# A float32 block on one TensorE: in units whose input is already whole, the high-weight products first, the low-weight products behind them

## The reference

```python
u = rmsnorm(x, norm_mix) * (1 + scale1) + shift1
aq, ak, av, bq, bkv, biq, bik, biw, cq, ck, cv, g = split_cols(u @ w_in)
y_a, y_b, y_c = diff_attention(...) @ w_br_a, dsa_attention(...) @ w_br_b, moba_attention(...) @ w_br_c
x = x + gate1 * ((sigmoid(g)-weighted sum of y_a, y_b, y_c) @ w_o)
x = x + gate2 * (square(relu(u2 @ w_ff1)) @ w_ff2)
...                                     # second block, two layers:
m = even_mixer(h) or odd_mixer(h)       # convolution and scan, or gated linear attention
h = layer_norm(ALPHA * h + m)
h = layer_norm(ALPHA * h + memory_cross_attention(h, mem, w_q, w_k, w_v, w_o))
h = layer_norm(ALPHA * h + square(relu(h @ w1)) @ w2)
```

## Time and profile before

| | |
|---|---|
| median of 3 runs | 2654.69 us (2653.97 to 2657.85) |
| the profiled execution | 2652.46 us |
| its span, first to last instruction | 2650.7 us |
| mean granted clock of TensorE | 0.992 |
| busy: PE, PEld, DVE, ACT, POOL | 98%, 81%, 56%, 44%, 16% of the span |
| HBM | 94 GB/s over the span |

### The profile page before, as it was taken

One profiled execution on the slowest core, in us unless ns is written; L12 is line 12 of the kernel. 1 busy time (PEld: TensorE's weight loads), 2 busy tenths in 40 slices (PEclk: granted clock), 3 DMA queues, 4 the chain that ended last, 5 costly groups with the idle time before them and its releaser, 6 DMA issues.

```text
span 2650.7 us, 34332 instructions
## 1 busy us (share of the span) xinstructions
PE 2595.9 (98%) x13569; PEld 2147.1 (81%) x13569; DVE 1493.1 (56%) x2875; ACT 1161.1 (44%) x2243; POOL 428.6 (16%) x508
## 2 busy tenths in 40 slices
PE   7999999999999999999999999999999999999998
PEld 5776677798888977887897988889788887888888
DVE  5176877565433389887774743335635744643334
ACT  4356554354232334554654542324533544542324
POOL 0133333100000045553000100000000100100000
PEclk8999999999999999999999999999999999999999
DMA  7342234434433333213421333332320432333331
GB/s 252 110 106 72 64 104 113 119 95 122 124 96 96 89 87 88 64 56 91 133 80 56 88 96 96 96 96 74 88 79 25 131 116 61 90 92 93 94 96 64
DMA packets 468976, 251.35 MB, mean 95 GB/s; under 512 B 15582, under 2 KB 463666, under 8 KB 468815
## 3 DMA queue, kind: packets, MB, share of 16 engines
q1 hardware_dynamic: 466260, 242.56, 32.0%
q0 software_dynamic: 1840, 5.59, 0.7%
q10 hardware_dynamic: 715, 1.01, 0.1%
HBM read 247.00 MB, written 2.13 MB: 94 GB/s over the span
## 4 chain that ended last, share of the span: by engine, by line
PE 86%; DVE 7%; ACT 3%; issue 3%; POOL 1%; DMA 0%; SPq 0%; DVEq 0%; POOLq 0%; ACTq 0%
PE ps L976 20%; PE ps L980 20%; PE ps L978 20%; PE ps L900 3%; PE ps L896 3%; PE ps L898 3%; DVE ps L2595 3%; PE ps L1130 1%; PE ps L914 1%; PE ps L916 1%; PE ps L1472 1%; PE ps L1494 1%; PE ps L927 1%; PE ps L1145 1%; DVE w_r L2475 1%
## 5 line engine op out<-in xcount | busy, mean ns | idle before, releaser
L976 PE MATMUL ps<-XH,wh 128*128 128x512 f32 (+2 forms) x1896 | 765.8, 404 | 7.3 <-ACT arena_f L1853 2.8
L980 PE MATMUL ps<-XH,w_r 128*128 128x512 f32 (+2 forms) x1896 | 750.1, 396 | 4.8 <-DVE w_r L2475 4.7
L978 PE MATMUL ps<-XL,wh 128*128 128x512 f32 x1776 | 704.6, 397 | 0.0
L2475 DVE TENSOR_TENSOR w_r<-w_f,wh 128x512 fp32r<-128x512 f32 (+1 forms) x625 | 409.1, 697 | 487.7 <-ACT wh L1648 486.9
L1648 ACT ACTIVATE wh<-w_f 128x512 fp32r<-128x512 f32 x787 | 445.8, 615 | 358.4 <-PE ps L980 204.0
L976 PEld LDWEIGHTS ps<-XH,wh 128*128 128x128 f32 (+2 forms) x1896 | 356.4, 188 | 112.5 <-issue 18.1
L980 PEld LDWEIGHTS ps<-XH,w_r 128*128 128x128 f32 (+2 forms) x1896 | 355.1, 187 | 92.3 <-DVE w_r L2475 7.8
L978 PEld LDWEIGHTS ps<-XL,wh 128*128 128x128 f32 x1776 | 332.8, 187 | 80.5 <-issue 4.3
L978 PE MATMUL ps<-arena_r,wh 128*128 128x512 f32 (+1 forms) x936 | 340.8, 364 | 0.1
L3599 POOL TENSOR_TENSOR w_r<-w_f,wh 128x256 fp32r<-128x256 f32 (+1 forms) x314 | 235.6, 780 | 326.3 <-ACT wh L1648 326.3
L976 PE MATMUL ps<-arena_r,wh 128*128 128x512 f32 (+1 forms) x726 | 265.6, 366 | 1.0 <-ACT wh L1648 1.0
(11 more groups left out here) (409 smaller groups left out, 3722.1 us busy)
## 6 DMA issues: line engine op xcount, KB each, us to landing
w_f<-in_mlp_w SPq DMA_DIRECT2D x126, 512.0 KB, 4.0
w_f<-in_w_ff SPq DMA_DIRECT2D x63, 512.0 KB, 4.0
w_f<-in_w_in SPq DMA_DIRECT2D x49, 512.0 KB, 3.9
w_f<-in_ada_w SPq DMA_DIRECT2D x35, 512.0 KB, 4.0
w_f<-in_even_w_in SPq DMA_DIRECT2D x35, 512.0 KB, 3.8
w_f<-in_odd_w_in SPq DMA_DIRECT2D x23, 512.0 KB, 3.8
w_f<-in_even_w_out SPq DMA_DIRECT2D x16, 512.0 KB, 4.1
w_f<-in_xa_w_v SPq DMA_DIRECT2D x16, 512.0 KB, 4.0
```

The lines of the kernel that those rows point to most:

```text
L976: e.matmul(b, hi[:, k, :], xh, start=u.first and k == 0, stop=False)
L978: e.matmul(b, hi[:, k, :], xl, start=False, stop=False)
L980: last = e.matmul(b, lo[:, k, :], xh, start=False, stop=u.final and k == u.kc - 1)
L2475: e.tensor_tensor(low[:, s], raw_[:, s], high[:, s], ALU.subtract).then_inc(dve.sem, dve.up("low", u.n, i))
```

## The change

`products` keeps a set of the inputs that an earlier call of `products` has run to their last chunk. For a call on such an input it runs the two high-weight products of all its chunks first and then the low-weight product of all its chunks. For a call on an input that is not in the set, the order stays chunk by chunk. The waits go with their products.

```diff
--- before.py
+++ after.py
@@ -962,24 +962,41 @@
                 else:
                     half_sums(st, 1)
 
+            whole_inputs = set()
+
             def products(us, part=None, ks=None):
 
                 if ks is None:
                     ks = range(us[0].kc) if part is None else range(part * KC // 2, (part + 1) * KC // 2)
                 outs = [(lin.of(*u.out) if ks[0] else bank_of(u))[0:u.cols, 0:u.tokens] for u in us]
-                for k in ks:
+
+                def high_products(k):
                     for u, b in zip(us, outs):
-                        hi, lo = chunks(high_flat(u), u.kc, u.cols), chunks(flat(u, 1), u.kc, u.cols)
+                        hi = chunks(high_flat(u), u.kc, u.cols)
                         xh, xl = chunk_of(u, k)
                         w.wait_ge(act, "high", u.n, piece_of(u, k, HIGH_PIECE))
                         w.wait_ge(act, "xh", u.x, k)
                         e.matmul(b, hi[:, k, :], xh, start=u.first and k == 0, stop=False)
                         w.wait_ge(dve, "xl", u.x, k)
                         e.matmul(b, hi[:, k, :], xl, start=False, stop=False)
+
+                def low_products(k):
+                    for u, b in zip(us, outs):
+                        lo = chunks(flat(u, 1), u.kc, u.cols)
                         w.wait_ge(low_by[u.low], "low", u.n, piece_of(u, k, LOW_PIECE[u.low]))
-                        last = e.matmul(b, lo[:, k, :], xh, start=False, stop=u.final and k == u.kc - 1)
+                        last = e.matmul(b, lo[:, k, :], chunk_of(u, k)[0], start=False, stop=u.final and k == u.kc - 1)
                         if k == u.kc - 1:
                             last.then_inc(pe.sem, pe.up("unit", u.n))
+
+                known = us[0].x in whole_inputs
+                for k in ks:
+                    high_products(k)
+                    if not known:
+                        low_products(k)
+                for k in ks if known else ():
+                    low_products(k)
+                if ks[-1] == us[0].kc - 1:
+                    whole_inputs.add(us[0].x)
 
             def ada_total(m):
```

## The result

The changed kernel takes 2642.12 us (median of 4 runs, 2640.48 to 2644.73) against 2655.32 us (4 runs, 2653.97 to 2657.85) for the kernel before: ratio 0.9949, 95% interval [0.9938, 0.9961]. The profiled execution's span went from 2650.7 to 2638.7 us, 12.0 less, at a mean granted clock of 0.991 against 0.992.

The account below looks back on a forecast made before the run. TensorE, busy 98% of the span, was taken as the bound: products times their spacing, plus stalls. Saved low-weight waits, high-weight waits and spacing summed as 2654.7 − 1.6 + 0 + 0 = 2653.1 us, range 2645 to 2664.

Parts of the forecast that it names:

- Term 3: Spacing of the 7272 reordered products on TensorE: taken as unchanged, 0, between ends of +9.2 and −6.6 us.
- three signs of being wrong: Full unit's low-weight stall behind the high run; high-weight wait at place 9; mean spacing moved by over 1 ns.
- lower end of −6.6 us: Every reordered wide product at the best raw slot's pace, 0.2313 us: 6552 × 1.0 ns = −6.6 us.
- second step of a set: High weight to the next high one in reordered units: spacing may rise as in L927, 1.6% over narrow units.
- third step: Low weight to low weight in reordered units: spacing may fall, as slow raw slots cost something; no separate size.
- Term 1: TensorE's waits for DVE's low weights in reordered units: 1.6 us saved, between ends of 0 and 2.8 us.
- the waits are all passed on: Rival: low-weight waits saved are stood at the next late producer; 2654.7 us, within no change; chance 0.15.
- Term 2: Second half of a unit's high weights wanted by product 9 instead of 13, 0.93 us sooner: covered, 0.
- The clock: Rival: one more or one less half-clock stretch of 3.4 us, costing 1.7 us; no chance given.
- The faster rival: High run in reordered units settles at the best raw slot's pace: −8.2 us, 2646.5 us; chance 0.22.

Follow-up runs that it names:

- e8: Kernel before, with all eight weight slots alike, 64 bytes below the inputs' place modulo 512 bytes: 2629.73 us, ratio 0.9903.
- e7: Changed kernel, high slots 32, 64 and 96 bytes above the inputs' place, arena and raw slots 128 bytes on: 2659.09 us, ratio 1.001.
- e1: Kernel before, with the raw slots moved to begin where the high slots do, modulo 512 bytes: 2628.18 us, ratio 0.9901.
- e12: e1 with a 32-byte pad ahead of the inputs, moving inputs and weights alike: 2632.62 us, ratio 0.9901.
- e10: Kernel before, with all eight weight slots alike, 96 bytes below the inputs' place modulo 512 bytes: 2668.62 us, ratio 1.005.
- e5: Kernel before, with all raw slots alike but 128 bytes from the high slots' place: 2647.57 us, a single run.
- e3: Changed kernel, known inputs running eight high products by XH, eight high by XL, then eight low: 2645.2 us, a single run.
- e4: Changed kernel, high run going over the chunks twice with inputs alternating, no weights used twice in a row: 2644.93 us, a single run.

## Why the prediction was wrong

**Term 3, the spacing, is the step that failed.** The text said "I take 0", the value between two ends, because two unknowns of opposite sign seemed of like size. Measured: −14.3 us for the pace of the reordered products, 2 ns each. Of the text's three signs of being wrong, a mean spacing moved by over 1 ns is the one that came. The lower end of −6.6 us was no bound either: it took the best raw slot's 0.2313 us for the floor, and that slot lay 128 bytes off. The floor, 0.2267, did not occur over a whole unit anywhere in the trace before. Sixteen of 24 products at 0.2267 against 0.2323 would be 6552 × 2/3 × 5.6 ns = 24 us; 13.2 came. The products behind a low run need a while to settle, as the unit at 1504.43 shows (3.66 us for its sixteen, against 3.63 at 1509.95), and the low run got no faster: the undisturbed feed-forward units gained (27.88 − 27.56) / 120 = 2.7 ns a product, which over 6552 would be 18 us. The other calls gained less. Calls of four chunks on XH and XL gained 0.2 ns a product, and the units on the scan's result, whose inputs lie 64 bytes off the high slots, gained nothing.

The observation that pointed to the truth stood in the text: "what TensorE reads has a small say in its pace", and five unit lengths that repeat with the five raw slots. I noted it and then did not ask what distinguishes the slots. Their spacing of 1032 words, and the high slots' of 1024, would have said it.

**The second step of a set "may rise as in L927".** It didn't. L927 and L1420 (now L1437) were wrong measures. e8 shows why for narrow chains: 0.120 is what narrow products take when weights and inputs lie at one place, 0.1133 when they are 64 bytes apart, whether high or low weights. L927 reads its high weights from the arena, which lies like XL, so its 0.1196 is that of the pair of buffers and not of high weights in a row: it stays at 0.120 in e8, which moved the slots but not the arena, and is 0.1185 in e7, which moved the arena by 128 bytes. The four of L1420 read the scan's result, which lies 64 bytes below their weights. In e8, where the two lie alike, they take 0.91 us instead of 0.94, 0.227 each, in the same order.

**The third step, low to low, "may fall".** It did not: 1.86 to 1.87 us for eight, 0.233, where the mean before was 0.2323.

**Term 1, the waits.** The forecast was that low-weight waits fall to about 5.6 us and high-weight waits stay at 2.9. They went to 3.5 and 7.1. No low weight is waited for in a reordered full unit any more, but the next new input's high weights are late instead: ACT was as close to the edge as DVE. The reordered calls did lose 1.5 us of waits, near the 1.6 of the forecast, but the first calls on a new input stand 1.5 us more, so the term is worth nothing. The rival "the waits are all passed on" was right on this term, and the three stretches that it named (504, 1294, 2102) hold the new or longer waits at 506, 1298 and 2120. Of the waits that were counted as gone, those at 1446 and 2239 came back as 0.34 and 0.33 us for high weights at 1443.94 and 2229.65; the one at 1903 did not.

**Term 2, high weights wanted earlier**, was right as put: no product at place 9 of a full unit stands in the list.

**The clock** was priced at 1.7 us for a stretch of 3.4 us more or less. The profiled execution after has 6.8 us more at half clock (17.1 against 10.2), by that price 3.4 us; in the calls of `products` it cost 1.8. The stretch at 510.8 became twice as long and one behind the wait at 1298 came new, while that at 1872.7 went. This is one execution of each kernel; in e1 and e12, in the old order, the low stretches lie elsewhere again (20.5 and 30.7 us in all).

**The faster rival** ("its weights always lie in the high slots and the odd raw slots are touched only in the low run") had the right mechanism and the wrong size: −8.2 us against −13.2. It got a chance of 0.22 since its counter-argument, that the low run still reads those slots, bears on a third of the products only.

**The rule from the Trainium skill** ("TensorE: Matmul & The Clock Gate", Back-to-back issue gap) is a formula with nothing but the number of columns in it, and gives 0.216 us. The section calls this the gap of a matmul by itself and puts a stream of weight loads and matmuls of 512 columns at about 0.131 us, which the prediction left out; it doesn't speak of operands. The rows show 0.2267 at the best placement and 0.2333 at the worst, so for these products neither figure is the pace, and the pace is not independent of what is read. The rule in "SBUF — State Buffer", Who interferes with whom, that weight loads and moving operands have ports of their own, does not describe this either: the distance between the two buffers changes the pace, in e10 against e1 with nothing but buffers moved, and within e1 between the units on XH (0.2267) and those on the scan's result (0.2333). What in the chip links the two reads no run here shows.

## What to carry over

Where TensorE is busy 98% of the time, look at the distance between the buffers it reads before the order in which it reads them: here a change of eight words of padding was worth 27 us of 2655, twice what the reordering gave, and made the reordering worth nothing. If units of equal work differ in length by the buffer they use, find what differs in the buffers; an order that seems to help may only be avoiding a bad one. And a wait removed at one late producer is no gain until the next one has been shown to have room.

## What the runs showed of the hardware

- The spacing of 128x512 float32r products depends on where weights and inputs lie to each other. It was 0.2267 us with weight buffers at the inputs' place (low weights there or 256 bytes off), 0.2288 with all weights 64 bytes below, 0.2312 with high weights at 0 and low ones 128 bytes off, 0.2333 at 32 or 96 bytes below and at 64 bytes above (e1 on the scan's result). Moving both by 32 bytes changed nothing.
- With 256 columns, 0 bytes apart is 0.120 us and 64 bytes apart, above or below, 0.1133, so the best place for narrow products is not the best for wide ones.
- A product's place acts on its neighbours. With low weights 128 bytes off (e5) the three steps of a set are 0.227, 0.232 and 0.234 us: the two beside the low product are slow. With raw slot 0 of the kernel before, 32 bytes off, all three are (0.233, 0.239, 0.229). In a run of their own the low products slowed that run and up to six products behind it (kernel after).
- It is indifferent to using the same weights twice in a row and to changing the input with each product (e3, e4: 27.56 us both).
- Only these distances were tried, on one kernel, with rows of 2048 bytes for the inputs' chunks and 512 for the weights'; whether other shapes have the same good places is open.
